# Feed-forward up tiles: one 512-column product for both input parts, with the two halves added afterwards

## What is computed

```python
def swiglu(x, w_gate, w_up, w_down):
    return (jax.nn.silu(x @ w_gate) * (x @ w_up)) @ w_down

for i in range(DEPTH_2):                      # 2
    f = swiglu(rmsnorm(h, ffn1_pre_g[i]), ffn1_w_gate[i], ffn1_w_up[i], ffn1_w_down[i])
    h = h + 0.5 * rmsnorm(f, ffn1_post_g[i])
    ...
    f = swiglu(rmsnorm(h, ffn2_pre_g[i]), ffn2_w_gate[i], ffn2_w_up[i], ffn2_w_down[i])
    h = h + 0.5 * rmsnorm(f, ffn2_post_g[i])
```

## Time and profile before

| | |
|---|---|
| median of 3 runs | 2963.75 us (2962.71 to 2965.57) |
| the profiled execution | 2961.03 us |
| its span (first to last instruction) | 2959.4 us |
| mean granted TensorE clock | 0.981 of full speed |
| busy: TensorE, weight loads, DVE, ACT | 2819.3, 2056.7, 1219.8, 951.5 us |

### The profile page before, as it was taken

One profiled execution on the slowest core, in us unless ns is written; L12 is line 12 of the kernel. 1 busy time (PEld: TensorE's weight loads), 2 busy tenths in 40 slices (PEclk: granted clock), 3 DMA queues, 4 the chain that ended last, 5 costly groups with the idle time before them and its releaser, 6 DMA issues. The chain is left out here.

```text
span 2959.4 us, 45725 instructions
## 1 busy us (share of the span) xinstructions
PE 2819.3 (95%) x18389; PEld 2056.7 (69%) x18389; DVE 1219.8 (41%) x1621; ACT 951.5 (32%) x1213; POOL 67.3 (2%) x130
## 2 busy tenths in 40 slices
PE   7989999999999999899999999999999999999998
PEld 5764444333343434399888988899899789989898
DVE  2553111111111111154584736545544864555544
ACT  2321111111111111154431645444543433463543
POOL 3010000000000000010000000100100000000000
PEclk9988999999999999999999999999999999999999
DMA  8586999999999999975443623555665345434552
GB/s 276 187 308 270 417 418 417 419 417 418 418 418 418 417 418 417 405 225 186 123 127 115 192 94 128 167 185 170 187 207 177 103 120 158 128 114 158 180 191 76
DMA packets 321680, 737.65 MB, mean 249 GB/s; under 512 B 14216, under 2 KB 234944, under 8 KB 283664
## 3 DMA queue, kind: packets, MB, share of 16 engines
q1 hardware_dynamic: 316784, 726.71, 66.9%
q0 software_dynamic: 4768, 9.12, 1.3%
HBM read 734.73 MB, written 1.05 MB: 249 GB/s over the span
## 5 line engine op out<-in xcount | busy, mean ns | idle before, releaser
L1475 PE MATMUL ps<-u_upper,w_lower 128*128 128x256 f32 x1984 | 523.8, 284 | 0.6 <-DVEq L2385 0.6
L465 PE MATMUL ps<-arena,ring 128*128 128x256 f32 x2304 | 510.9, 382 | 1.2 <-DVE arena L447 1.2
L465 PEld LDWEIGHTS ps<-arena,ring 128*128 128x128 f32 x2304 | 436.0, 191 | 62.6 <-issue 3.6
L1475 PE MATMUL ps<-u_upper,w_upper 128*128 128x256 f32 x1408 | 401.4, 285 | 3.4 <-DVE u_lower L1883 3.4
L1475 PE MATMUL ps<-u_lower,w_upper 128*128 128x256 f32 x1408 | 400.2, 284 | 0.0
L1877 DVE TENSOR_TENSOR w_lower<-ring,w_upper 128x2048 fp32r<-128x2048 f32 x128 | 293.3, 2292 | 216.2 <-ACT w_upper L1842 216.2
L1512 PE MATMUL ps<-arena 128*64 128x512 f32 x1632 | 366.2, 599 | 13.9 <-DMA arena<-in_exp_w_up 13.9
L1475 PEld LDWEIGHTS ps<-u_upper,w_lower 128*128 128x128 f32 x1984 | 368.8, 193 | 1.4 <-DVEq L2385 1.4
L1628 DVE TENSOR_SCALAR arena<-ps 128x512 f32<-128x512 f32 x34 | 23.5, 692 | 790.3 <-PE ps L1512 790.3
L1842 ACT ACTIVATE w_upper<-ring 128x2048 fp32r<-128x2048 f32 x128 | 244.8, 1913 | 196.4 <-PE ps L1475 196.4
L1512 PEld LDWEIGHTS ps<-arena 128*64 128x64 f32 x1632 | 110.2, 137 | 252.6 <-issue 198.6
(11 more groups left out here) (582 smaller groups left out, 3371.1 us busy)
## 6 DMA issues: line engine op xcount, KB each, us to landing
arena<-in_exp_w_up SPq DMA_DIRECT2D x204, 1024.0 KB, 20.3
ring<-in_exp_w_down SPq DMA_DIRECT2D x136, 1024.0 KB, 22.4
ring<-in_w_in SPq DMA_DIRECT2D x75, 1024.0 KB, 5.8
ring<-in_exp_w_up SPq DMA_DIRECT2D x68, 1024.0 KB, 24.1
ring<-in_ffn_w_gate SPq DMA_DIRECT2D x44, 1024.0 KB, 5.4
ring<-in_ffn_w_up SPq DMA_DIRECT2D x44, 1024.0 KB, 5.4
ring<-in_ffn_w_down SPq DMA_DIRECT2D x44, 1024.0 KB, 4.9
ring<-in_ada_w SPq DMA_DIRECT2D x24, 1024.0 KB, 10.5
```

The lines of the kernel that those rows point to most:

```text
L465: ins = nc.tensor.matmul(bank(b, 2, TOK)[:, m, :], w[:, k, m * P:(m + 1) * P], rhs[:, k, :], start=(k == 0 and (part is None or (part == 0 ...
L1475: ins = nc.tensor.matmul(out_, w_ if w_is_lhs else x_, x_ if w_is_lhs else w_, start=start and n == 0, stop=stop and n == 2, skip_group_ch ...
```

## The change

The input's upper and lower parts now lie side by side in one buffer `u_both`, 256 + 256 columns for each depth. Upper weights by both is one product of 512 columns into a whole bank: the first half of the bank gets upper by upper, the second half upper weights by lower input. The lower weights by the upper input, 256 columns, are added to the first half. So a tile takes two banks (one for each 128 of its columns), a chunk all four, and TensorE waits ahead of each up tile until DVE has freed its banks. The two halves of a bank are added outside TensorE: ACT copies the second halves of a tile to a buffer `rest`, DVE adds them to the first halves. The gate's sum goes to `gated`, where ACT applies silu in place; the up tile's sum goes to `hidden`, where DVE multiplies. The third weight split of a chunk on DVE now comes ahead of the product of the hidden values.

```diff
-            alias("second_0", 4096)
+            u_both = alias("u_both", 4096, F32R)
...
-        UH, UL = view(0, KT, TOK, of=u_upper), view(0, KT, TOK, of=u_lower)
+        U2 = view(0, KT, 2, TOK, of=u_both)
+        UH, UL = U2[:, :, 0, :], U2[:, :, 1, :]
+        rest = view(27712, 2, 2, W)
...
 def ffn_up_pe(pe, T, T0, rnd, b, strip=None):
...
+                both = ps[:, b + m, :]
                 for k in range(KT):
                     if strip and m == 0:
                         strip(k)
-                    ins = passes_mm(bank(b, 2, TOK)[:, m, :], wh[:, k, c], wl[:, k, c], UH[:, k, :], UL[:, k, :],
-                                    True, k == 0, k == KT - 1, False)
+                    nc.tensor.matmul(both, wh[:, k, c], U2[:, k, :, :].rearrange("p a b -> p (a b)"), start=(k == 0),
+                                     stop=False, skip_group_check=True)
+                    ins = nc.tensor.matmul(both[:, 0:TOK], wl[:, k, c], UH[:, k, :], start=False, stop=(k == KT - 1),
+                                           skip_group_check=True)
...
 def ffn_pe(pe, T0, r, nf):
...
             ffn_up_pe(pe, T0, T0, r, 4, strip)
-            ffn_up_pe(pe, T0 + 1, T0, r, 5)
+            ffn_up_pe(pe, T0 + 1, T0, r, 6)
...
-                b = 4 + 2 * ((c4 + 1) % 2)
                 if not last:
-                    ffn_up_pe(pe, T0 + 2 + 3 * c4, T0, rnd, b)
-                    ffn_up_pe(pe, T0 + 3 + 3 * c4, T0, rnd, b + 1)
+                    pe.wait_ge(sem("ffn_sums"), nf * 2 * NCH + 2 * c + 1)
+                    ffn_up_pe(pe, T0 + 2 + 3 * c4, T0, rnd, 4)
+                    pe.wait_ge(sem("ffn_sums"), nf * 2 * NCH + 2 * c + 2)
+                    ffn_up_pe(pe, T0 + 3 + 3 * c4, T0, rnd, 6)
...
 def ffn_act(act, T0, r, nf, n, gain, extra=None):
...
+            def copy_rest(up):
+
+                nc.scalar.activation(rest[:, up, :, :], ps[:, 4 + 2 * up:6 + 2 * up, TOK:2 * TOK], ACT.Copy).then_inc(
+                    sem("ffn_rest"), 1)
+
+            act.wait_ge(sem("tile_mm"), nf * NT + 2)
+            copy_rest(0)
+
             def chunk(c, c4, rnd, last):
...
-                act.wait_ge(sem("tile_mm"), nf * NT + 3 * c + (2 if c4 else 3))
-                b = 4 + 2 * (c4 % 2)
-                nc.scalar.activation(gated[:, c4 % 2, :, :], bank(b, 2, W), ACT.Silu).then_inc(sem("ffn_silu"), 1)
+                act.wait_ge(sem("ffn_sums"), nf * 2 * NCH + 2 * c + 1)
+                g = gated[:, c4 % 2, :, :]
+                nc.scalar.activation(g, g, ACT.Silu).then_inc(sem("ffn_silu"), 1)
                 if not last:
                     upper(3, first + 1, T0 + 3 + 3 * c4, rnd)
+                act.wait_ge(sem("tile_mm"), nf * NT + 3 * c + (2 if c4 else 3))
+                copy_rest(1)
                 act.wait_ge(sem("ffn_hidden"), nf * NCH + c + 1)
...
                     upper(4, first + 2, T0 + 4 + 3 * c4, rnd)
+                    act.wait_ge(sem("tile_mm"), nf * NT + 3 * c + 4)
+                    copy_rest(0)
...
 def ffn_dve(dve, T0, r, nf, n, gain, extra=None):
...
+            def sums(n, up, dst):
+
+                dve.wait_ge(sem("ffn_rest"), nf * 2 * NCH + n)
+                v.tensor_tensor(dst, ps[:, 4 + 2 * up:6 + 2 * up, 0:TOK], rest[:, up, :, :], ALU.add).then_inc(
+                    sem("ffn_sums"), 1)
+
+            sums(1, 0, gated[:, 0, :, :])
+
             def chunk(c, c4, rnd, last):
...
-                dve.wait_ge(sem("ffn_silu"), nf * NCH + c + 1)
-                v.tensor_tensor(hidden[:, par, :, :], gated[:, par, :, :], bank(5 + 2 * par, 2, W),
-                                ALU.mult).then_inc(sem("ffn_hidden"), 1)
                 if not last:
                     lower(3, first + 1, T0 + 3 + 3 * c4)
+                sums(2 * c + 2, 1, hidden[:, par, :, :])
+                dve.drain()
+                dve.wait_ge(sem("ffn_silu"), nf * NCH + c + 1)
+                v.tensor_tensor(hidden[:, par, :, :], gated[:, par, :, :], hidden[:, par, :, :],
+                                ALU.mult).then_inc(sem("ffn_hidden"), 1)
                 dve.drain()
...
                     lower(4, first + 2, T0 + 4 + 3 * c4)
+                    sums(2 * c + 3, 0, gated[:, 1 - par, :, :])
```

## The result

| | before | after |
|---|---|---|
| median (20 runs each) | 2963.2 us (2958.3 to 2967.99) | 2958.07 us (2952.25 to 2963.3) |
| the profiled execution | 2961.03 us | 2962.34 us |
| its span | 2959.4 us | 2960.7 us |
| mean granted TensorE clock | 0.981 | 0.978 |

The ratio is 0.9984, with a 95% interval of 0.9976 to 0.9992: faster by 5.1 us, 0.17%. The prediction was 2950, 13.7 us less. Its direction holds, its size does not: less than half came.

A forecast was written before the change was run, and what follows sets the result against it. The prediction took TensorE, busy 95% of the span, to bound the kernel. Products -17.2, tail +3.0, head +0.5 and steady chunks 0 gave -13.7 us, applied to the median 2963.75: 2950 us, range 2943 to 2957.

The forecast's parts named there:

- The products, -17.2 us: In up and gate tiles, one 512-column product replaces two of 256, saving 12.5 ns per step: -17.2 us.
- the lower bound: Smallest saving allowed for the products: a 512-column product at 235 ns saves 5 ns per step, -6.9 us.
- The tail, +3.0 us: At each stage's end, the new DVE sum lengthens the chain TensorE waits for: 4 x 0.76 us.
- The head, +0.5 us: At each stage's start, ACT's new copy delays the second gate tile's weights: TensorE waits 0.13 us, 4 times.
- Each stage begins at the lower clock: At each stage's start, about 7 steps, 28 in all, run at the lower clock and save nothing.
- Steady chunks, 0: In steady chunks, the new copies and sums stay hidden, with cover of 4 us and more: no added time.
- The rival in which TensorE waits for its banks: At gate or up tile starts, TensorE waits 1.6 us for sums, once per chunk: 64 us, 3014 us; chance 0.05.
- The likeliest case's weak edge: Least gain in the forecast case (chance 0.83): 10 ns saved per step, ends up to +7 us, 2957 us.
- that rule's 2964: For TensorE's products, a fixed cost of 2.5 ns each saves 3.5 us, which the stage ends eat: 2964 us.

The follow-up runs named there:

- experiment 1: The changed kernel with each up tile's 16 products of 512 columns first, then its 16 of 256: 2952.95 us, ratio 0.9964 against the kernel before.
- experiment 2: The changed kernel with the lower weights multiplied by both input parts too, so all 32 products of an up tile have 512 columns: 3097.08 us, ratio 1.0453.
- experiment 11: The changed kernel run once more with no edit: 2954.35 us, ratio 0.9983 against the kernel before.
- experiment 6: The changed kernel with the last down tile's weights split ahead of the last copy and sum: 2952.18 us, ratio 0.9956 against the kernel before.
- Experiments 6 and 7: 7 is the kernel before the change with the last down tile's weights split early: 2955.09 us, ratio 0.9973; experiment 6 has its own line.
- experiment 8: The changed kernel with each of the 88 sums on DVE made twice: 2968.15 us, ratio 1.002 against the kernel before.
- pairs: The changed kernel with products in the order 512, 512, 256, 256 columns: 2956.14 us, ratio 0.9974 against the kernel before.
- the bank (4): The changed kernel with each short product adding into the other bank than the long one before it, except in a stage's first tile: 2955.97 us, ratio 0.9982.

## Why the prediction was wrong, step by step

**The products, -17.2 us: the step that failed.** It priced the 512-column product by "227.5, the mean over a whole tile", a tile in which every product has 512 columns. In the changed up tile it stands between products of 256 columns, and there it is followed after 233 to 241 ns and a step takes 353 ns, not 347.5. 7 ns are saved per step, not 12.5. By ACT's timeline an up tile gives back 0.11 us, 88 of them 9.7 us. The prediction had the right row before it, "the slowest pair of starts is 1373.41 to 1373.88 for two, 235 ns each", and used it as the lower bound. These are the two starts behind short products: the row was not the slow end of a spread, but the price for just this neighbourhood. Experiments 1 and 2 show that the neighbours are what matters: in runs of one length the same product is followed after 226.7 ns.

**Two terms that were missing.** The down tiles stand behind the changed stream, and their code is untouched, so they were given 5.46 us as before. They took 5.50 by TensorE's timeline, against 5.47 before, 0.033 x 44 = 1.5 us. And the prediction put everything outside the stages at nothing. In the profiles with the change each mixer is longer, by 0.8 and 1.1 us in experiment 11 and by 4.4 and 4.6 in the first profile, at a lower granted clock.

**The tail, +3.0 us: right.** 6.3 us of waits instead of 3.3, and experiment 6 shows that they are paid in full. Experiments 6 and 7 together give 2.8 by the stages.

**The head, +0.5 us: not found.** No such wait of TensorE is in the list. ACT's timeline in stage 2 has the order that was forecast:

```profile
1921.93 0.60 ACT L1860 ACTIVATE arena<-ps 128x512 f32<-128x512 f32 x1 [2.70 <-PE ps L1774]
1922.55 1.28 ACT L1848 ACT_TABLE_LOAD   x1
1923.84 1.92 ACT L1848 ACTIVATE w_upper<-ring 128x2048 fp32r<-128x2048 f32 x1
```

The tile behind which the copy stands ends at 1921.73, and copy, table load and upper weights are done at 1925.76, 4.0 us later, as forecast. DVE's lower weights and the first product that needs them:

```profile
1925.79 2.29 DVE L1895 TENSOR_TENSOR w_lower<-ring,w_upper 128x2048 fp32r<-128x2048 f32 x1 [2.54 <-ACT w_upper L1848]
...
1928.19 0.47 PE L1772 MATMUL ps<-u_both,w_upper 128*128 128x512 f32 x1
```

They are done at 1928.08, 0.11 us ahead of it, which is the hand-over: just in time, not 0.13 us late. "Each stage begins at the lower clock" was read from one stage and is not so in every one (28 steps were taken out of the sum for it, 0.35 us): in stage 2 of before nearly all starts behind the first product lie 120 ns apart.

**Steady chunks, 0: right.** TensorE never waited for the sums, even with each sum doubled (experiment 8). The rival in which TensorE waits for its banks did not come.

**Sum.** -9.7 + 1.5 + 3.0 + 0 = -5.2 us. That it meets the -5.1 measured between medians is in part luck: these are terms of the stages alone, and four times stage 2 gives -6.3. The mixers take 1.9 of that back in experiment 11 and more in the first profile; how much on average the runs don't show. The forecast of 2950 was 8 us too low, and the measured 2958.07 lies 1 us above the range's upper end of 2957. The likeliest case's weak edge allowed a step's saving of 10 ns at least; the 7 ns that came lie between that and the 5 ns of its own bound.

**The fixed cost of a product.** The prediction set the Trainium skill's rule (about 2.5 ns over the columns, "TensorE: Matmul & The Clock Gate", section "Wait — 56ns, not 53.3ns?") against the trace. The median, 2958.07, lies nearer to that rule's 2964 than to the forecast, but for another reason. Experiments 1 and 2 have 226.7 and 120.0 ns in runs of equal length, 13.3 ns above the columns at 2.4 GHz (213.3 and 106.7) in both. A cost that is the same at both lengths it is, as the Trainium skill has it, but more than five times its 2.5 ns. In alternation two products carry 352.5 - 320.0 = 32.5 ns, not 26.7, and experiment 1 gets nearly all of that difference back.

**What stays open.** Why a long product behind a short one is late, why pairs keep a quarter of the loss and not half, and why a run of long ones needs five to ten starts to settle. The change of length can't be the whole cause: behind the wait at the end of stage 2 of before, where all products are long, the starts lie 332, 224, 231, 236, 228, 233 and 231 ns apart and only then 227. The operands (experiment 2) and the bank (4) are excluded. The order of the weight loads was not examined. Why the mixers are longer behind changed stages is open too.

## What to carry to other kernels

Price an operation from a row in which its neighbours are those that it will have, not from the mean over a tile of its own kind; and where TensorE must run products of two lengths, group them by length, which here gave 5 us for a changed order, though a stage's first tile, whose operands still come in one by one, lost 0.8 us by it. At a stage's end, look for work that is ready early and stands behind work that is late: that split was worth as much again. A wait there that grows can cost the clock as well as its own length. Where single profiled spans scatter by more than the change is worth, compare the stages, each from its first to its last product, and then the unchanged parts behind them too, which here gave back some of the gain.

## What the runs showed of the hardware

- In runs of one length products start 226.7 ns apart at 512 columns and 120.0 at 256 (experiments 1 and 2). From 512 to 256 columns some 7 ns are gained (starts of 113 and 119 ns); from 256 to 512 a run of long ones starts some 27 ns late in all, spread over five starts, or some 63 ns over ten behind an alternating stream (224 to 241 ns instead of 226.7). A run of long ones that begins behind a wait starts late in the same way.
- The lower clock came after a wait of 2.33 us in a busy stage (427 ns instead of 227 for some starts), not after one of 1.57 us in the same place (experiment 8 and the changed kernel, all four stages of each).
- Executions of one kernel differ by stretches at the lower clock (4 us in a mixer of the changed kernel), and the time follows the mean granted clock. In the runs of before beside the experiments, 17 with a mean clock of 0.981 average 2961.97 us, and 3 with 0.978 average 2967.0. At equal clock the changed kernel is the faster by more than the medians tell: 2952.97 (7 runs) against 2961.97 at 0.981, 2960.7 (4 runs) against 2967.0 at 0.978. Its runs have a lower clock on average, 0.9793 against 0.9804. The profiles show one place of it, the mixers (experiment 11); its cause they don't show.
